# First four input tiles of an mLSTM block taken over the inner dimension from outside, and small block-diagonal loads issued by ScalarE

## What is computed

```
cond = silu(c)
mod  = cond @ ada_w[0] + ada_b[0]            # c (1, 1024), ada_w[0] (1024, 6144)
sh_m, sc_m, ... = split(mod, 6)
u    = x * (1.0 + sc_m) + sh_m               # x (256, 1024)
xm, z = split(u @ w_in, 2)                   # w_in (1024, 4096)
xc   = silu(causal_depthwise_conv(xm, conv_w, conv_b))
q, k = block_diag_proj(xc, wq), block_diag_proj(xc, wk)   # 512 blocks of 4 x 4
v    = block_diag_proj(xm, wv)
gates = q @ wg_q + k @ wg_k + v @ wg_v + b_gates
```

## Time and profile before

| | us |
|---|---|
| median of three | 2766.47 (2764.12 to 2769.9) |
| profiled execution | 2763.41 |
| its span | 2761.5 |
| TensorE busy | 2676.0 |
| VectorE, ScalarE, POOL busy | 781.9, 403.7, 754.9 |

### The profile page before, as it was taken

The page is one execution under the profiler, slowest core; times in us unless marked ns, Lnnn a source line. Parts: engine busy times, 40 slices in busy tenths (PEclk is TensorE's granted clock), DMA queues, the critical chain, the costliest instruction groups (busy, mean ns, idle before and its releaser), DMA issues.

```text
span 2761.5 us, 52666 instructions
## 1 busy us (share of the span) xinstructions
PE 2676.0 (97%) x23469; PEld 1974.1 (71%) x23469; DVE 781.9 (28%) x1499; ACT 403.7 (15%) x828; POOL 754.9 (27%) x585
## 2 busy tenths in 40 slices
PE   7999999989999999999999999999999989999999
PEld 5767888857655555655555445478888878998998
DVE  3315310064300000000002395142221136532651
ACT  0032010020300000000002245110000021221100
POOL 0041055074000000000000170045555332621886
PEclk9999999999999999999999999999999999999999
DMA  9968544478599999999997410142222233122552
GB/s 302 310 240 274 140 159 152 154 256 278 169 371 382 386 379 382 380 380 391 376 378 276 110 61 1 61 138 84 85 92 84 84 122 107 62 77 80 171 163 92
DMA packets 375157, 565.41 MB, mean 205 GB/s; under 512 B 50152, under 2 KB 205584, under 8 KB 374800
## 3 DMA queue, kind: packets, MB, share of 16 engines
q1 hardware_dynamic: 351504, 554.58, 57.9%
q10 hardware_dynamic: 23424, 7.42, 1.1%
HBM read 557.75 MB, written 1.05 MB: 202 GB/s over the span
## 4 chain that ended last, share of the span: by engine, by line
PE 56%; issue 35%; POOL 3%; DVE 2%; POOLq 2%; ACT 1%; DMA 1%; DVEq 1%; SPq 0%; ACTq 0%
PE psum L994 13%; PE psum L1833 10%; PE psum L2052 5%; PE psum L1870 5%; PE psum L1914 3%; PE psum L1160 3%; PE psum L2080 2%; PE psum L1310 2%; PE psum L1934 2%; PE psum L1651 2%; PE psum L1035 1%; PE psum L1961 1%; POOLq L3658 1%; DMA ring<-in_ada_w 1%; POOLq L3556 1%
## 5 line engine op out<-in xcount | busy, mean ns | idle before, releaser
L1509 PE MATMUL psum<-ring,xe 128*32 128x256 f32 x8448 | 467.3, 380 | 4.2 <-DMA ring<-in_moe_w 2.8
L1509 PEld LDWEIGHTS psum<-ring,xe 128*32 128x32 f32 x8448 | 270.0, 110 | 187.9 <-issue 9.7
L994 PE MATMUL psum<-act_in,ring 128*128 128x256 f32 x1216 | 270.0, 383 | 1.3 <-DVE act_in L2627 1.1
L994 PEld LDWEIGHTS psum<-act_in,ring 128*128 128x128 f32 x1216 | 231.9, 192 | 41.3 <-issue 8.9
L3657 POOL TENSOR_TENSOR ckv<-ckv,nstat 128x512 f32<-128x512 f32 x2 | 2.5, 1262 | 923.5 <-DVE nstat L3202 923.5
L1533 PE MATMUL psum<-ring,zs 128*32 128x256 f32 x4224 | 237.3, 379 | 2.8 <-DMA ring<-in_moe_w 2.2
L3112 DVE TENSOR_TENSOR zs<-zs,psum 128x128 f32<-128x128 f32 x132 | 37.9, 287 | 643.7 <-ACT zs L2362 643.6
L1533 PEld LDWEIGHTS psum<-ring,zs 128*32 128x32 f32 x4224 | 136.7, 110 | 95.3 <-DMA ring<-in_moe_w 6.2
L3670 POOL TENSOR_TENSOR w_sums<-ring 128x512 f32<-128x512 f32 (+1 forms) x34 | 42.2, 1242 | 301.6 <-DVE ctxT L3259 126.8
L1651 PE MATMUL psum<-a,ring 128*128 128x512 f32 x224 | 97.5, 594 | 2.0 <-ACT a L2412 1.3
L2362 ACT ACTIVATE zs<-psum 128x128 f32<-128x128 f32 x132 | 36.6, 278 | 391.9 <-PE psum L1509 391.9
(11 more groups left out here) (552 smaller groups left out, 4201.0 us busy)
## 6 DMA issues: line engine op xcount, KB each, us to landing
ring<-in_moe_w SPq DMA_DIRECT2D x320, 512.0 KB, 8.4
ring<-in_ffn_w SPq DMA_DIRECT2D x97, 1024.0 KB, 5.2
ring<-in_ada_w SPq DMA_DIRECT2D x96, 1024.0 KB, 7.6
ring<-in_moe_w SPq DMA_DIRECT2D x88, 1024.0 KB, 10.1
ring<-in_hg_w_in SPq DMA_DIRECT2D x20, 1024.0 KB, 5.1
ring<-in_mlstm_w_in SPq DMA_DIRECT2D x16, 1024.0 KB, 6.2
ring<-in_moe_w SPq DMA_DIRECT2D x64, 256.0 KB, 5.5
ring<-in_mlstm_w_out SPq DMA_DIRECT2D x8, 1024.0 KB, 7.4
```

Source lines behind the costliest of these rows:

```text
L994: last = pe.matmul(bank(j)[:, n * T:(n + 1) * T], tile[:, k * width + n * P:k * width + (n + 1) * P], src(k), start=start and k == 0, stop ...
L1509: last = pe.matmul(psum[32 * g:32 * g + 32, r, 0:2 * P].rearrange("p (u n) -> p u n", u=2), xe[:, 2 * i + k, at:at + 32], tile[:, k, :, g ...
```

## The change

The input weights of the first four output tiles (the first 1024 of w_in's columns) are loaded as four tiles of 256 rows by 1024 columns, m_row0 to m_row3. The ada projection is done in four steps of 256 channels, each with both their shift and their scale columns: ada tiles a0 a0, m_row0, a1 a1, m_row1 and so on. Each ada step ends its own accumulation, ScalarE copies the row after each, outer_columns turns it, outer_modulate modulates two chunks of act_in, and outer_products adds the product of those two chunks to each of four banks. A bank holds one of the four tiles through all four rounds. ScalarE issues the late parameters in three portions, each behind a copy. VectorE forms lanes after the modulations. The ada tiles are now each loaded by two DMAs, in pieces of 256 columns.

The eight small loads leave SP. ScalarE issues the four of k_blocks after its copy of input tile 3, and the three of qkv_small and wgates after that of tile 4. The waits for them are unchanged. The rest of the diff adjusts counts.

```diff
-TILES = [("ada_a", 8), ("m_in0", FIRST_INPUT)]
+OUTER_INPUT = 4
+TILES = []
+for _s in range(ADA_STEPS["a"]):
+    TILES += [(f"ada_a{_s}", 2), (f"m_row{_s}", 1)]
+TILES += [(f"m_in{OUTER_INPUT}", FIRST_INPUT - OUTER_INPUT)]
...
-JOBS = [("params", 1), ("xT", 4), ("late_params", 4), ("m_in", 8 + EARLY_Z), ("m_fold", 4), ...
+JOBS = [("params", 1), ("xT", 4), ("m_outer", OUTER_INPUT), ("late_params", 4), ("m_in", 8 + EARLY_Z - OUTER_INPUT), ("m_fold", 4), ...
...
             def stage_ada0():
-                ada(tile_of["ada_a"], w["ada_w"][0], 0, 8)
+                for s in range(ADA_STEPS["a"]):
+                    for half in range(2):
+                        t = tile_of[f"ada_a{s}"] + half
+                        if t >= RING:
+                            sp.wait_ge(tile_begun, t - RING + 2)
+                        rows = w["ada_w"][0][4 * half * P:4 * (half + 1) * P].rearrange("(c p) n -> p c n", p=P)
+                        dst = ring[:, t % RING].rearrange("p (c i n) -> p c i n", c=4, i=2)
+                        for i in range(2):
+                            sp.dma_start(dst[:, :, i], rows[:, :, i * D + 2 * P * s:i * D + 2 * P * (s + 1)]
+                                         ).then_inc(loaded[t % RING], 16)
+                    load_rows(tile_of[f"m_row{s}"], w["mlstm_w_in"][0][:, 0:D], 2 * P * s)
...
-                for j in range(16):
+                for j in range(OUTER_INPUT, 16):
                     load_cols(in_tile(j), w["mlstm_w_in"][0], 256 * j, 256)
...
-                    if j == 3:
-                        for i, name in enumerate(("mlstm_wq", "mlstm_wk", "mlstm_wv")):
-                            src = w[name][0].rearrange("(c n) i o -> (n i) c o", n=32)
-                            sp.dma_start(qkv_small[:, i], src).then_inc(S("mlstm_small_in"), 16)
-                        k_rows = w["mlstm_wk"][0].rearrange("(c n) j o -> n c (j o)", n=32)
-                        for i in range(4):
-                            sp.dma_start(k_blocks[i:P:4], k_rows).then_inc(S("mlstm_small_in"), 16)
-                        sp.dma_start(wgates[:], w["mlstm_w_gates"][0].rearrange("(c p) g -> p c g", p=P)
-                                     ).then_inc(S("mlstm_small_in"), 16)
...
+            def outer_columns(s):
+
+                pe.wait_ge(S("mod_rows_out"), s + 1)
+                for m in range(4):
+                    last = pe.matmul(psum[:, 7, 4 * s + m:4 * s + m + 1], mod_rows[:, m * P:(m + 1) * P],
+                                     c_("pick")[:, s:s + 1], start=True, stop=True)
+                last.then_inc(S("mods_full"), 1)
+
+            def outer_products(s, j):
+
+                if j == 0:
+                    wait_tile(pe, tile_of[f"m_row{s}"])
+                    pe.wait_ge(S("mlstm_in_ready"), 2 * s + 2)
+                if s == 0:
+                    wait_free(pe, in_job(j))
+                tile = ring[:, tile_of[f"m_row{s}"] % RING].rearrange("p (c n) -> p c n", c=2)
+                for n in range(2):
+                    for k in range(2):
+                        last = pe.matmul(bank(in_job(j))[:, n * T:(n + 1) * T], tile[:, k, (2 * j + n) * P:(2 * j + n + 1) * P],
+                                         act_in[:, 2 * s + k], start=s == 0 and n == 0 and k == 0,
+                                         stop=s == OUTER_LAST and k == 1, skip_group_check=True)
+                        if j == 0 and n == 0 and k == 0:
+                            last.then_inc(tile_begun, 1)
+                if s == OUTER_LAST:
+                    full(last, in_job(j))
+                elif j == OUTER_INPUT - 1:
+                    last.then_inc(tile_begun, 2)
...
             def stage_ada0():
-                for i in range(ADA_STEPS["a"]):
-                    ada_step("a", i, 1)
+                turn_x(0)
+                ada_step("a", 0, 1)
+                turn_x(1)
+                turn_x(2)
+                outer_columns(0)
+                turn_x(3)
+                for s in range(OUTER_LAST):
+                    outer_products(s, 0)
+                    outer_products(s, 1)
+                    ada_step("a", s + 1, 1)
+                    outer_products(s, 2)
+                    outer_columns(s + 1)
+                    outer_products(s, 3)
+                for j in range(OUTER_INPUT):
+                    outer_products(OUTER_LAST, j)
                 pe.wait_ge(S("late_params_in"), 16 * (len(prow_dmas) - FIRST_PARAMS))
                 for g in range(4):
                     turn(job_of["late_params"] + g, [prow[:, 1 + g, :]])
-                ada_columns("a", 0, 1)
...
             def stage_ada0():
+                late = prow_dmas[FIRST_PARAMS:]
+                for s in range(OUTER_LAST):
+                    act.wait_ge(S("ada_full"), s + 1)
+                    if s:
+                        act.wait_ge(S("mods_full"), s)
+                    act.activation(mod_rows, psum[:, 6, :], ACT.Copy).then_inc(S("mod_rows_out"), 1)
+                    for dst, src in late[s::OUTER_LAST]:
+                        act.dma_start(dst, src).then_inc(S("late_params_in"), 16)
+                act.wait_ge(S("mods_full"), OUTER_LAST)
                 mod_rows_out("a")
...
                         out_of(act.activation(xm[:, 2 * i:2 * i + 2, 4:4 + T], src, ACT.Copy), j)
+                        if i == OUTER_INPUT - 1:
+                            k_rows = w["mlstm_wk"][0].rearrange("(c n) j o -> n c (j o)", n=32)
+                            for r in range(4):
+                                act.dma_start(k_blocks[r:P:4], k_rows).then_inc(S("mlstm_small_in"), 16)
+                        elif i == OUTER_INPUT:
+                            for r, name in enumerate(("mlstm_wq", "mlstm_wk", "mlstm_wv")):
+                                rows = w[name][0].rearrange("(c n) i o -> (n i) c o", n=32)
+                                act.dma_start(qkv_small[:, r], rows).then_inc(S("mlstm_small_in"), 16)
+                            act.dma_start(wgates[:], w["mlstm_w_gates"][0].rearrange("(c p) g -> p c g", p=P)
+                                          ).then_inc(S("mlstm_small_in"), 16)
...
+            def outer_modulate(s):
+
+                dve.wait_ge(S("mods_full"), s + 1)
...
             def stage_ada0():
+                for g in range(3):
+                    x_out(g)
+                outer_modulate(0)
+                x_out(3)
+                for s in range(1, OUTER_LAST + 1):
+                    outer_modulate(s)
...
                 for g in range(4):
                     params_out(job_of["late_params"] + g, 1 + g)
-                ada("a", 0, 0, 0, 4)
```

More of the change, by code:

```diff
@@ L294, in build_program @@
         more_loads[tile_of["mla_in"] + 2] = 1
+        more_loads.update({tile_of[f"ada_a{s}"] + half: 1 for s in range(ADA_STEPS["a"]) for half in range(2)})
         more_loads.update({tile_of["mla_uq"] + i: 3 for i in range(4)})
@@ L354, in in_job @@
         def in_job(j):
[L356 removed]
+            if j < OUTER_INPUT:
+                return job_of["m_outer"] + j
+            return job_of["m_in"] + j - OUTER_INPUT if j < 8 + EARLY_Z else job_of["m_z"] + j - 8 - EARLY_Z
         def step_job(name, i):
@@ L1027, in ada_half @@
                 r = s % batch
-                ends = r == batch - 1 or s == ADA_STEPS[stage] - 1
+                ends = stage == "a" or r == batch - 1 or s == ADA_STEPS[stage] - 1
                 t, width = ada_tile(stage, s), n * batch
@@ L1036, in ada_half @@
                                      ring[:, (t + k // 4) % RING, (k % 4) * BANK:(k % 4 + 1) * BANK],
-                                     start=r == 0 and k < 4, stop=ends and k >= 4, skip_group_check=True)
-                    if k % 4 == 0:
+                                     start=(stage == "a" or r == 0) and k < 4, stop=ends and k >= 4, skip_group_check=True)
+                    if k % 4 == 0 and (stage != "a" or s == 0):
                         last.then_inc(tile_begun, 1)
@@ L1210, in stage_mlstm @@
             def stage_mlstm():
-                for j in range(16):
-                    mm_pair(in_tile(j), in_job(j), lambda k: act_in[:, k],
-                            before=(lambda k: pe.wait_ge(S("mlstm_in_ready"), k + 1)) if j == 0 else None)
+                for j in range(OUTER_INPUT, 16):
+                    mm_pair(in_tile(j), in_job(j), lambda k: act_in[:, k])
                     if FIRST_INPUT - 1 <= j < FIRST_INPUT - 1 + UNDER_INPUT:
@@ L2713, in stage_prep, with x_out @@
                 params_out(job_of["params"], 0)
[L2714 to L2721, removed]
+            def x_out(g):
+                j = job_of["xT"] + g
+                wait_full(dve, j)
+                out_of(dve.tensor_copy(xT[:, 2 * g:2 * g + 2], bank(j).rearrange("p (a t) -> p a t", a=2)), j)
+            def outer_modulate(s):
+                dve.wait_ge(S("mods_full"), s + 1)
+                pair = slice(2 * s, 2 * s + 2)
```

(16 more changed lines are left out.)

24 lines of the change are left out of this document (12 added, 12 removed).

## The result

The changed kernel takes 2781.3 us, median of six (2779.4 to 2785.4), against 2764.9 for six runs of before (2762.9 to 2769.9). The ratio is 1.0055, with a 95% interval from 1.0045 to 1.0065. The forecast was 2763.1, no measurable change, with a range from 2756.5 to 2770.0. The profiled execution has a span of 2778.5 us against 2761.5, 17.0 more.

What follows compares the result with a forecast made beforehand. TensorE, busy 97% of the span, was taken as the bound, so its idle time and waits count. Front -10.4, stall +5.0, clock dip +2.0 gave -3.4 us: from the median 2766.5 to 2763.1, range 2756.5 to 2770.0.

Steps and rivals of the forecast that it cites:

- part 2: Small loads moved to ScalarE: their later landing holds VectorE's chain and then TensorE before z tile 10; 5.0 us lost.
- The stall of 5.0: TensorE's idle time before z tile 10, waiting for VectorE's first gate fold; range 1.2 to 6.6 us, 5.0 taken.
- the dip behind the wait: TensorE's clock falls to half after a stall or the early front's gaps; 2.0 us lost, counted once.
- nearer to the upper half: Choice within the stall's range before z tile 10, whose upper end was landing 75.5, stall 6.6; 5.0 taken.
- Rival C: Small pieces and ring pieces take turns; landing about 86, stall 17.1, net +8.7, 2775.2 us; chance 0.11.
- The front: Interleaved ada and row tiles fill TensorE's early idle time; input tile 4 begins at 54.0, not 64.4; gain 10.4 us.
- rival D: Sparse work up to 23 us lowers TensorE's clock; front products cost 5 us more; +1.6, about 2768; chance 0.12.
- r2 and r3: Third and fourth row tiles of input weights, waiting for ring space until 27.0 and 35.9; loads hardly pause.
- the sum's three places: Front gain, stall before z tile 10 and clock dip: -10.4 + 5.0 + 2.0 = -3.4 us.

Runs made afterwards that it cites:

- e2: The kernel before, with only the eight small loads moved from SP to ScalarE behind its copies of input tiles 3 and 4; 2780.5 us, ratio 1.0058.
- e5: e3's kernel, with TensorE multiplying zeros by zeros between its pieces of work in the front; 2754.4 us, ratio 0.9951.
- e12: The kernel before, unchanged, profiled once more; span 2761.4 us against 2761.5 in its first profile.
- e4: The changed kernel, unchanged, profiled once more in a single execution; 2776.4 us, span 2774.5.
- e6: The changed kernel, unchanged, timed again on the same chip as other runs; median of five 2785.9 us, ratio 1.0065.
- e3: The changed kernel, with VectorE doing the convolution ahead of the block diagonals, small loads still on ScalarE; 2757.8 us, ratio 0.9961.
- e1: The changed kernel, with the eight small loads back on SP, between row tile 3 and input tile 4; 2769.9 us, ratio 1.0011.

## Why the prediction was wrong

**The step that failed** is the duration of the small loads, in part 2 of the sum. I took 11.5 us from the first issue of the second four to the landing, 14.5 with a ring tile beside them, and a landing at 72.5 to 75.5. It was 22.3 us (65.47, right behind the copy of tile 4, to 87.77). The stall of 5.0 was 14.6. Everything else of that part came out as worked out: 39.6 us from landing to z tile 10 where I had 39.2, and the dip behind the wait 2.1 where I had 2.0.

Why it was undersized: the pace was read rightly, from a stretch where the small loads had the engines for themselves, but I let only ring tile 18 and the rest of 17 run beside them, 3.0 us. SP's issues in the changed kernel, and the queues from 74 to 76 us (q10 is ScalarE's):

```profile
73.34 0.37 SPq L777 DMA_DIRECT2D ring<-in_mlstm_w_in  x1
74.20 1.36 SPq L777 DMA_DIRECT2D ring<-in_ada_w  x2
```

```profile
q10 hardware_dynamic: 2586, 0.08, 69.6%
q1 hardware_dynamic: 95, 0.10, 15.2%
```

With the ring nearly idle the small pieces went at 1293 a us, and by 75.6 about three quarters of the 12288 had passed beside the one ring tile of the forecast; at that pace the other 3200 would have been through by about 78, some 12.5 us after the first issue (an estimate from these two numbers). But the ada step behind tile 5 and then tile 6 let SP issue three more tiles, 3 MB, from 73.3 on. From 76 on each small piece waited for a ring piece of 1 or 2 KB, the pace fell to 370, 239 and 175 a us (76 to 82, by 2 us), and the last 3200 pieces took until 87. A second, smaller part is ScalarE's own issue of the four loads: 7.2 us (65.47 to 72.70) where I allowed 3 to 6 and called it harmless, so wgates was issued only at 71.81. For the 1.4 us from issue to first byte the prediction gives no row; the first 16-byte piece moved at 66.51, 1.0 us after its issue. My row of the load that took 9.3 us for 4096 pieces was nearer: 12288 pieces at that pace would be 28 us, against 22.3 measured. I had used it as "nearer to the upper half" of a range whose upper end left it out.

**Rival C** was this mechanism, in its place and with its point of decision (82.4 us). Its prices: landing 86 for 87.8, stall 17.1 for 14.6, 2775.2 for 2781.3. It had a chance of 0.11, for a bad reason: I set the total of pieces moved in a 32 us window against it, and a total over a window with idle time in it says nothing about who waits for whom. The page's rule of the Trainium skill that stood beside it (DMA: Bandwidth & Descriptors, Queues, rings and completion order), that each engine goes round the queues that have work, a packet at a time, is borne out; the grain measured here is one piece, 351 to 351 and 870 to 868, never more than 4 apart. The other rule I named, that issuing from another engine saves only sequencer time, isn't contradicted, but leaves out what counted: moving the loads changed what they waited for, and e2 prices that at 12 us.

**The front** was oversized: 6.0 us, not 10.4. Products began at 19.4 and not 17.4, with both ada halves ahead of them at half the pace (1.94 us), and the first sixteen records, some of them at half the pace too, took 5.1 and not 3.5 us; e5, without that, begins tile 4 3.3 us earlier. A round takes 9.85 (24.42 to 34.27: 5.29 and 1.92 for products, 1.85 for the ada step, 0.79 for the columns). My own terms add up to 9.2, but the sum went on by 8.9 a round: two ada steps were entered at 1.7 and 1.5 us instead of the 1.85 read, so the forecast of tile 4 should have been 54.5 by its own terms. My rival D had the slow front at 5 us; here it was part of the outcome, not an alternative, and its sign, a granted clock near 0.5 between 18 and 40, did not show: the profile reads 1.00 there. That the loads keep pace, that ScalarE's copies and late loads hide, and that r2 and r3 are no bound held: the chain shows no DMA and no ScalarE between 19 and 57.

**What would it take to have it right:** with -6.0, 14.6 and 2.1 in the sum's three places it would have been +10.7, 2776 to 2777. That leaves about 5 us of the measured median unexplained.

**What stays open:** some 6 us of the first profile's 17.0 were lost behind 181 us. Part are longer stretches of low clock at places where the kernel before has them too. The changed kernel around 2250, and e12, the kernel before, at the same place:

```profile
2240.00:2262.00 22.00, 19.64 (x71) 0.75 0.50 161
```

```profile
2223.00:2245.00 22.00, 19.29 (x69) 0.77 0.50 161
```

In the first profile of before the same place (2227 to 2249) reads 0.92. Behind 190 us the granted clock is 0.50 for 65.2 us in the changed kernel, 63.6 in e4 and 68.6 in e6, against 58.2 and 61.6 in the two profiles of before: 7.0 us more in the first pair, which at half pace cost about 3.5 of the 6 us (an estimate). In e4 the same kernel ended only 13.0 us above before's first span, with z tile 10 7.1 us late. The dips do come back at the same places, as e4 was to find out, but their lengths move, without any change to the kernel too. Whether the changed kernel has more of them by chance, or by where a shift of 11 us puts the work, was not settled.

## What to carry over

Before moving a load to another queue, find the engine that waits for it and follow its work to the critical engine: here 39 us of VectorE's work lay behind a landing, and doing the part that doesn't need the load first (e3) gained 10 us on before, where the same change without it lost 16. Price a load made of tiny pieces by the number of pieces of the other queue that pass meanwhile, not by its bytes or by its pace alone. And when TensorE is brought forward by some us, list everything that had slack against it: e1 fails at the tile behind the same eight loads, e2 and the changed kernel at the work behind their landing.

## What the runs showed of the hardware

- The DMA engines take one piece of SP's queue and one of ScalarE's in turn while both have work: 351 and 351 in 2 us with pieces of 2 KB against 32 bytes, 870 and 868 with 512 bytes against 32, never more than 4 apart.
- Small pieces of ScalarE's queue moved at 1293 a us while the ring was nearly idle (74 to 76 us), and at 175 a us beside ring pieces of 2 KB (80 to 82 us).
- Four times as many ring pieces for the same bytes lowered the ring's pace from 0.69 to 0.43 MB in 2 us beside such small pieces.
- A wait of 14.6 us of TensorE had 2.1 us more behind it, at a granted clock of 0.50 that lasted until about 131.
- In the front of the changed kernel the ada halves ran at half pace (1.94 us) while the profile's granted clock read 1.00; with the idle time filled (e5) they took 1.06. A short idle piece by itself doesn't do it: before, an ada half behind 1.64 us of idle time took 1.07.
